# Second attention: where GpSimd multiplies a finished pair of heads by its gate and stores it

## The reference

```python
q = rmsnorm(q, q_g) / 8;  k = rmsnorm(k, k_g)            # per head
for blk in range(8):                                      # blocks of 128 queries
    z = q[blk] @ k[:kend].T                               # only keys up to the block's end
    log_keep = where(strict, log_sigmoid(-z), 0)
    suffix   = reverse_cumsum(log_keep) - log_keep
    weights  = where(strict, exp(log_sigmoid(z) + suffix), 0)
    out      = weights @ v[:kend]
return (o * silu(gate)) @ w_out
```

## Time and profile before

| | us |
|---|---|
| median of 3 runs | 3135.73 (3134.46 to 3139.21) |
| the profiled execution | 3134.45 |
| its span | 3133.0 |
| TensorE busy | 3042.1 (97%) |
| VectorE busy | 1839.8 (59%) |
| ScalarE busy | 1396.3 (45%) |
| GpSimd busy | 660.6 (21%) |
| `weigh`, L2796, 128 times | 161.1 |
| one pair of the second attention, 2397.66 to 2475.91 | 78.25 |

### The profile page before, as it was taken

One profiled execution on the slowest core, in us unless ns is written; L12 is line 12 of the kernel. 1 busy time (PEld: TensorE's weight loads), 2 busy tenths in 40 slices (PEclk: granted clock), 3 DMA queues, 4 the chain that ended last, 5 costly groups with the idle time before them and its releaser, 6 DMA issues. The chain is left out here.

```text
span 3133.0 us, 39543 instructions
## 1 busy us (share of the span) xinstructions
PE 3042.1 (97%) x15324; PEld 2541.0 (81%) x15324; DVE 1839.8 (59%) x2502; ACT 1396.3 (45%) x2104; POOL 660.6 (21%) x444
## 2 busy tenths in 40 slices
PE   8999999999999999999999999998999999998998
PEld 6888888888888878787887878877878888886787
DVE  4444223666666634367667576676557777777544
ACT  5333213555555423335244252443346666666531
POOL 0210002222223200302010020110235555544210
PEclk9999999999999999999999999998999999999999
DMA  3111222211112234112121121211121111112422
GB/s 111 52 47 49 67 74 68 74 55 61 55 55 67 81 120 147 53 36 81 41 74 54 41 81 48 74 48 61 34 101 41 41 41 41 39 42 75 155 99 76
DMA packets 58807, 208.44 MB, mean 67 GB/s; under 512 B 6928, under 2 KB 9872, under 8 KB 58512
## 3 DMA queue, kind: packets, MB, share of 16 engines
q1 hardware_dynamic: 49360, 174.16, 16.5%
q0 software_dynamic: 9280, 31.99, 3.3%
HBM read 170.87 MB, written 26.87 MB: 63 GB/s over the span
## 5 line engine op out<-in xcount | busy, mean ns | idle before, releaser
L119 ACT ACTIVATE whi<-wraw 128x1024 fp32r<-128x1024 f32 x208 | 218.4, 1050 | 418.5 <-PE a_D L132 64.2
L124 DVE TENSOR_TENSOR wlo<-wraw,whi 128x1024 fp32r<-128x1024 f32 x173 | 237.5, 1373 | 156.7 <-ACT whi L119 155.6
L130 PE MATMUL ssm_D<-x1hi,whi 128*128 128x512 f32 x640 | 257.5, 402 | 0.0
L130 PE MATMUL b_D<-x1hi,whi 128*128 128x512 f32 x640 | 254.1, 397 | 0.0
L132 PE MATMUL ssm_D<-x1hi,wlo 128*128 128x512 f32 x640 | 250.5, 391 | 0.0
L131 PE MATMUL ssm_D<-x1lo,whi 128*128 128x512 f32 x640 | 250.4, 391 | 0.0
L132 PE MATMUL b_D<-x1hi,wlo 128*128 128x512 f32 x640 | 250.2, 391 | 0.0
L131 PE MATMUL b_D<-x1lo,whi 128*128 128x512 f32 x640 | 249.9, 391 | 0.0
L2644 DVE TENSOR_TENSOR_SCAN stick_keep<-stick_keep,stick_first 128x896 f32<-128x896 f32 (+7 forms) x128 | 214.6, 1680 | 41.9 <-ACT stick_keep L2531 41.4
L2796 POOL TENSOR_TENSOR stick_rows<-stick_rows,stick_keep 128x896 f32<-128x896 f32 (+7 forms) x128 | 161.1, 1261 | 257.8 <-DVE stick_keep L2644 241.6
L130 PE MATMUL a_D<-x1hi,whi 128*128 128x512 f32 x512 | 201.8, 394 | 12.3 <-DVE x1lo L159 12.3
(11 more groups left out here) (458 smaller groups left out, 7680.3 us busy)
## 6 DMA issues: line engine op xcount, KB each, us to landing
wraw<-w_dram SPq DMA_DIRECT2D x208, 512.0 KB, 3.6
sq<-acum_rows SPq DMA_DIRECT2D x32, 512.0 KB, 3.8
att_bias<-alibi_dram SPq DMA_DIRECT2D x16, 512.0 KB, 3.8
stack<-stack POOLq DMA_DIRECT2D x32, 256.0 KB, 3.7
f<-y_b SPq DMA_DIRECT2D x11, 512.0 KB, 5.7
x_sb<-xT_dram SPq DMA_DIRECT2D x8, 512.0 KB, 8.8
branch_a<-sq POOLq DMA_DIRECT2D x8, 512.0 KB, 3.5
y_b<-att_y POOLq DMA_DIRECT2D x8, 512.0 KB, 3.0
```

The source lines that it names most:

```text
L119: act.activation(self.whi[:, s, :, :], self.wraw[:, s, :, :], ACT.Copy).then_inc(self.w_hi, 1)
L124: dve.tensor_tensor(self.wlo[:, s, :, :], self.wraw[:, s, :, :], self.whi[:, s, :, :].bitcast(F32), ALU.subtract).then_inc(self.w_lo, 1)
L130: pe.matmul(out, self.whi[:, s, w0, :], xhi[:, k, cols], start=start, stop=False)
```

## The change

For every pair but the last, `output` and `store` leave the end of the pair and are issued in the next pair, behind `weigh` of its row 0 and ahead of `weigh` of its row 1. The last pair keeps its `output` at its end (its `store` does nothing). No instruction is added or taken away, and no other engine's list changes.

```diff
                 for slot in range(19):
                     if slot < 16:
                         weigh(p, slot)
+                    if slot == 0 and p > 0:
+                        output(p - 1, 1 - q)
+                        store(p - 1)
                     if slot == 1:
                         gate(p, q)
...
                         stack_parts(p + 1, 1 - q)
-                output(p, q)
-                store(p)
+                if not more:
+                    output(p, q)
+                    store(p)
```

## The result

The changed kernel takes 3171.0 us (3169.34 to 3171.66, 4 runs) against 3137.47 us (3134.46 to 3139.81) for the kernel before in the same comparison: ratio 1.0108, 95% interval 1.0096 to 1.0120. It is slower by 1.1%, about as forecast (3170). The span of the profiled execution went from 3133.0 to 3170.1 us, 37.1 more.

A forecast was written before the change was run, and what follows sets the result against it. TensorE's list was taken to bound six pairs. Delay 21.6, clock 9.9 and last pair 3.0 sum to 34.5 us; on 3134.45 that gives 3169.0, with the median 1.3 above: 3170 us, range 3146 to 3180.

The forecast's parts named there:

- The bound: In six pairs TensorE's list sets the time; its wait before the first two rows' turn, 0.96 us, leaves no cover.
- the old place costing nothing: At the pair's end, multiply and store do not hold the first row up; GpSimd idles 0.83 us behind them.
- Steps 1 to 3: Change of pairs: first row's scan takes 2.03 us for 2.53; second scan ends 2406.74; moved multiply stands behind it, ending 2409.01.
- Step 4: Third row's scan stands until 2409.01, ends 2409.30; VectorE then issues the weight tile's low part about 2409.95, ending 2411.16.
- Step 5: After the store (2410.21) the low part goes first; second row weighed at 2413.03 for 2409.40, delay 3.6 us.
- my own second branch: GpSimd's weighing of the second row goes before VectorE's low part: weighed at 2412.25, delay 2.85 us.
- Step 6: Behind the second row: gate multiply takes 2.4 instead of 3.39 us, third row is not late next, TensorE stays the bound.
- The clock: Behind the longer idle time ahead of the turn TensorE's clock falls to 0.50: 6 x 1.65 = 9.9 us.
- The last pair: Seventh change of pairs: same steps without an evacuation, so the low part ends 0.63 us earlier; delay 3.0 us.
- the first rival's order: The moved multiply goes ahead of the waiting second scan; second row weighed 1.9 us later, total 3159 us, chance 0.15.
- a lower clock costs nothing new here: In the last pair a clock fall adds nothing, since its mean granted clock is 0.89 already.
- three signs of being wrong: Multiply shown with 2.4 us; turn waiting under 3 us; pair lengthened less than the turn's wait grows.

The follow-up runs named there:

- the filler run: The changed kernel plus 28 TensorE products with unused results ahead of the turn of the first two rows, in six pairs: 3178.53 us, ratio 1.0135.
- three reciprocals: The changed kernel plus three small unused reciprocals on VectorE ahead of the weight tile's low part in slot 2: 3175.88 us, ratio 1.0122.

## Why the prediction was right, and where it was not

*The bound, and the old place costing nothing:* right. Moving the store alone changes nothing; filling 0.68 us of the turn's wait with work shortens the pair by 0.61.

*Steps 1 to 3, the first row's scan freed and the multiply standing:* right. 2.02 for 2.03, and 4.38 for "about 4.4", in all six.

*Step 4:* right but for the low part's end; the scan is shown with 2.11, the low part issued at 2410.13 less the 0.25 of shift, for 2409.95.

*Step 5, who goes first at 2410:* wrong. The rule read from the trace, that the one that waits longest goes first, did not hold here. I let the low part take the way 0.3 us ahead of the weighing, for a delay of 3.6. The weighing went first and was 2.8 later, close to the 2.85 of my own second branch. The price came back with more: behind a DMA issue GpSimd's weighing, gate multiply and scale kept the way, and the low part ended at 2417.70 (2417.45 without the shift) instead of 2411.16.

*Step 6, what comes behind shrinks and TensorE stays the bound:* wrong. The low parts of the rows' weights are late, which the step does not look at, and the values start 5.5 us later than before (2418.40 less 0.25, for 2412.67), whatever TensorE does in between.

*The clock:* the fall and its price were right, 1.57 and 1.60 us where it shows, for 1.65. But in the changed kernel it costs nothing: it falls in each of the six pairs, and twice as long in the second, and they are alike within 0.06 us. Two pairs with the clock at 1.00 show it directly: the first of the filler run (83.97 us) and the fifth with three reciprocals (83.99). What the low clock costs is hidden in the time in which the values are awaited anyway.

*The last pair:* 2.9 us for 3.0, by other steps. The clock had fallen earlier here, the second row's scan was issued 0.25 us behind the multiply, and so the multiply went first (2.35 us): the first rival's order, in this pair alone. The second row was weighed at 2915.28, or 2881.39 less the pair's shift of 33.89, for 2879.48: 1.9 later, as that rival has it, and not 3.0. The other 1.0 us came behind it, with the granted clock down from 0.89 to 0.84 and TensorE busy 64.65 instead of 62.35 us. The sentence that a lower clock costs nothing new here is not borne out; which part is the clock's was not measured. That the term comes out at 2.9 is luck.

So the sum, 34.5 forecast for 37.1, comes near by two errors that offset each other, which is luck: the delay at the values (5.7 us a pair with what follows) was put at 3.6, and 1.65 of clock was added that was hidden. Together that is 5.25 a pair. None of the three signs of being wrong that the prediction names came up, though two of its readings were off: the second row is weighed in 2.01 us and not 2.8, and the turn waits 3.76 us and not 4.6. What it had right, the multiply standing behind the scan, gives the later turn: 2.8 us of the 5.7.

**Still open:** why VectorE is passed over behind a DMA issue. A DMA issue with idle time behind it does not do so: with 1.75 us in the run with the store alone, and with 1.10 us in the last pair of the changed kernel, the low part took the way at the weighing's end. In all runs in which it is kept out, VectorE gets the way at the same place, behind the scale of the weight tile and ahead of the third row's weighing, whether two ends of GpSimd's instructions were passed before (changed kernel) or one (both behind the second row). Time does not sort them either: VectorE is still passed over 4.96 us behind the start of the DMA issue in the changed kernel (2414.76 − 2409.80) and gets the way 4.88 us behind it in the other (2417.00 − 2412.12). Nor is it the transfer alone: it lands 3.0 us from its issue, at 2412.80, and VectorE is passed over once more at 2414.76. So the runs show that the store directly ahead decides, and not by what mechanism.

## What to carry to other kernels

- Before moving an instruction to "behind" another, measure the gap there and ask what the other engine on the shared way does in it: 3.6 us of work were moved into 2.8 us beside a running scan.
- A gap on an engine that waits for a neighbour is not free if the moved work holds that neighbour up.
- When a wait lowers the clock and a second wait follows, keep the engine busy through the first: if the second wait grows by what the clock gives back (0.93 to 2.53 us here), the low clock cost nothing.

## What the runs showed of the hardware

- GpSimd's and VectorE's instructions with two operands in SBUF excluded each other for their whole length: the multiply of 2.4 us is shown with 4.38 behind a scan, and a standing low part finishes 1.08 us behind the other's end where its own time is 1.21. The lengths of steps 2 and 3 followed from this.
- Directly behind a DMA issue on GpSimd's queue, VectorE's standing instruction was passed over at one or two ends of GpSimd's instructions (low part shown with 7.57, 6.30 and 5.68 us, scan with 3.88); without the DMA issue there it was not (low part 2.23).
- The granted clock fell to 0.50 behind an idle time of TensorE of 3.76 us in all six pairs of the changed kernel, but in only five of six with three reciprocals (3.77 us). Behind 2.6 us it fell in five of six pairs with the store behind the second row and in four of six with it behind the gate multiply. A fall cost 1.57 and 1.60 us where nothing else was awaited, and nothing where the values were awaited anyway.
